# The expert loop in another order: each expert's down projection behind the next expert's gate and up

## The chip, the cores and the metric

The kernel runs on one core of a Trainium2 chip, as one launch. The metric is the time of one execution on the device in microseconds (us). The time of the kernel before is the median of three runs.

## The reference

One step of a small encoder trunk for two request groups (256 prompt frames and 32 sample frames, 288 tokens of 1024 features). It has two layers: an mLSTM and retention mixer, then a mixture of experts; a gated DeltaNet mixer, then a second mixture of experts. The change touches the two mixtures alone:

```python
def hier_moe(x, w_grp, b_grp, w_exp, b_exp, w_gate, w_up, w_down):
    """x (N,D): top-1 expert group, then top-2 experts inside it; only selected experts are evaluated."""
    ...
    def expert_block(args):
        xb, e = args
        hb = jax.nn.silu(xb @ w_gate[e]) * (xb @ w_up[e])
        return hb @ w_down[e]
    ...
    y = out_rows[dest] * gw_s[:, None].astype(x.dtype)
    return jax.ops.segment_sum(y, tok_s, num_segments=n)
```

There are 32 experts. Each has a gate and an up matrix of 1024 x 512 and a down matrix of 512 x 1024, all in float32, so each matrix is 2048 KB and each mixture reads 96 of them from device memory.

## The kernel before

**Blocks.** Tokens are held in slots of 32 per expert (`BLK`), and a block `b` is four experts (`QUAD`), numbered 4b to 4b+3. With the inputs of this case a mixture is eight blocks, each expert once. In the text expert 31 is the last of a mixture, and `u` is an expert's place in its block. The first block is written out, the others are a loop on each engine.

**TensorE (PE), for each block.** `gather` picks the block's token rows with one-hot products. Then for each of four experts: `gate_up(u, b)` multiplies 32 tokens by the gate and the up matrix (32 products each, it begins when both matrices are there); `flip_hidden(u, b)` transposes the hidden rows; `down(u, b)` multiplies by the down matrix (16 products). `scatter(b)` adds the block's rows to the tokens with five groups of products, and DVE adds them into `X`. Between `gate_up` and `flip_hidden` ScalarE (ACT) takes the SiLU and VectorE (DVE) multiplies by up (`hidden`); between `flip_hidden` and `down` DVE copies the flipped rows (`hidden_T`). After `down`, DVE and ACT copy the result to `ys` (`outputs`).

**The matrices.** Six ring slots of 2048 KB hold the matrices of two experts: expert i+2 is loaded into the slots of expert i (`RING_SLOT`; the first three experts have further slots, `FIRST_SLOT`). The loads are issued by SyncE's queue (SP), in program order: gate, up, down of one expert, then of the next. Each waits until its slot is read: on `gate_used`, `up_used` or `down_used`, which PE raises at the end of the gate half, of `gate_up` and of `down`.

**The ends of a mixture.** A mixture ends with `down(3, 7)`, its `outputs`, `scatter(7)` and DVE's adds. The first mixture is followed by the second layer's norm and input products, whose first four weight pieces SP loads into ring slots right behind expert 31's matrices (`pieces`). The second mixture is followed by the final norm and the stores.

**Where the first block differs.** In block 0 PE has `share_rows`, three products that spread the routing rows, behind the first `down`; DVE makes the next block's one-hot and this block's shares (`onehot(0)`, `shares(0)`) behind the first expert. In the trace the 32-wide hidden tiles are named `zT`, ring slots `W`, and PE's products stand at line 343, a helper.

Of the kernel before, what the change touches and what calls it, by code (L numbers as in the profile page):

```python
# [16 lines left out]
ACT = mybir.ActivationFunctionType  # L17
X_AXIS = mybir.AxisListType.X

P = 128  # L20
# [11 lines left out]
BLK = 32  # L32
QUAD = 4
# [104 lines left out]
def trunk(nc, a):  # L138

    with ExitStack() as ctx:  # L140
# [200 lines left out]
        def _(pe):  # L341
# [696 lines left out]
            def experts(l):  # L1038
# [148 lines left out]
                def expert(u, b):  # L1187
                    gate_up(u, b)
                    flip_hidden(u, b)
                    down(u, b)  # L1190
# [23 lines left out]
        def _(act):  # L1214
# [295 lines left out]
            def experts(l):  # L1510
# [34 lines left out]

                def iteration(b):
                    fetched(b)
                    for u in range(QUAD):
                        i = 4 * b + u
                        act.wait_ge(m["gate_used"], i + 3)  # L1550
                        nc.scalar.activation(sg[u % 2], banks[2 + u % 2][0:64, 0:2 * P], ACT.Silu  # L1551
                                             ).then_inc(m["silu"], 1)
                        act.wait_ge(m["down_used"], i + 3)
                        if u == 0:
                            act.wait_ge(m["scattered"], SCATTERS * b + SCATTERS)
                        for c in (2, 3):
                            ins = nc.scalar.copy(ys[BLK * u:BLK * u + BLK, 256 * c:256 * c + 256],  # L1557
                                                 banks[5 + u % 2][BLK * c:BLK * c + BLK, 0:256])
                            ins.then_inc(m["y_act"] if c == 3 else part_done, 1)
# [21 lines left out]
        def _(dve):  # L1581
# [710 lines left out]
            def experts(l):  # L2292
# [133 lines left out]
                def expert(u, b):  # L2426
                    i = 4 * b + u
                    hidden(u, i)
                    hidden_T(u, i)
                    outputs(u, i)  # L2430

# [39 lines left out]
                expert(0, 0)  # L2471
                for t in range(TILES):
                    n, bank = N_TOK[t], banks[(4, 6, 7)[t]]
                    E["rows_wide"].wait(dve)
                    cp(rows[:, :, P * t:P * t + n], bank[:, 0:4 * n].rearrange("p (j n) -> p j n", j=4))
                onehot(0)
                shares(0)
                for u in range(1, QUAD):
                    expert(u, 0)
                adds(0)  # L2480
                nb = nblk_reg(dve)
                with dve.Fori(1, nb) as b:
                    fetched(b)
                    expert(0, b)
# [345 lines left out]
```

## Time and profile before

| | |
|---|---|
| median of three runs | 1464.29 us (1462.56 to 1466.79) |
| the profiled execution, its own time | 1455.58 us |
| its span, from first to last instruction | 1453.7 us |
| PE busy | 1155.0 us (79%) |
| DVE busy | 470.4 us (32%) |
| ACT busy | 252.1 us (17%) |
| queue of SP's loads | 448.35 MB, 76.7% of 16 DMA engines |
| PE's mean granted clock | 0.903 |

The profiled execution is 8.7 us below the median of the three runs; sums are made against its own time. Busy shares are means over stages with different limits: the two mixtures and the two mixers have to be read apart, and a busy PE is not a PE at its peak, since products are pipelined and four narrow ones run side by side. The granted clock has two levels here, 1.00 (2.4 GHz) and 0.50 (1.2 GHz); a stretch that holds both shows a mean between them.

### The profile page before, as it was taken

What the parts mean: (1) busy time and instruction counts of PE and PEld (TensorE: products, weight loads), DVE (VectorE), ACT (ScalarE), POOL (GpSimd) and SP (SyncE); (2) the same over time, 40 slices, a digit from 0 to 9 for tenths busy, and PEclk for the clock granted to TensorE, in tenths of its full rate; (3) what the DMA queues carried; (4) which work ended last, traced back from release to release, by engine and by line L of the source; (5) the groups of instructions that cost most, each with busy time, mean ns of one, the idle gap of its engine ahead of it and who ended that gap; (6) DMA issues with size and microseconds to landing.
All of it is one profiled execution on the core that took longest, in us unless ns stands there. A gap on an engine that the chain in (4) does not pass through costs nothing.

```text
span 1453.7 us, 27532 instructions
## 1 busy us (share of the span) xinstructions
PE 1155.0 (79%) x11710; PEld 716.8 (49%) x11710; DVE 470.4 (32%) x1210; ACT 252.1 (17%) x636; POOL 65.7 (5%) x100
## 2 busy tenths in 40 slices
PE   8999889887686775776899989898866768778665
PEld 6645547444353443443578666656534434344342
DVE  1024355432232221322343746535222213222133
ACT  2122214110010110101222414231110101011011
POOL 2001102100000000000200101011000000000001
PEclk9999999988787898887999999898999978788898
DMA  9852236999999999999833303148999999999995
GB/s 278 171 105 81 109 123 249 424 410 428 428 427 430 427 429 429 428 429 427 277 117 116 118 4 131 60 182 341 410 427 429 428 428 429 427 430 428 428 429 218
DMA packets 54146, 453.87 MB, mean 312 GB/s; under 512 B 5680, under 2 KB 6480, under 8 KB 29760
## 3 DMA queue, kind: packets, MB, share of 16 engines
q1 hardware_dynamic: 52176, 448.35, 76.7%
q0 software_dynamic: 1904, 4.58, 1.1%
q8 instruction: 49, 0.80, 0.2%
q14 instruction: 17, 0.14, 0.0%
HBM read 449.55 MB, written 3.35 MB: 312 GB/s over the span
## 4 chain that ended last, share of the span: by engine, by line
PE 57%; DMA 31%; DVE 6%; issue 3%; ACT 1%; SPq 1%; POOL 1%; DVEq 0%; ACTq 0%; POOLq 0%
PE bank L343 56%; DMA W<-in_moe_w_up 30%; PE bank L346 1%; DMA W<-in_ab_w_in 1%; DVE zT L2402 1%; ACT zT L1551 1%; SPq L2554 1%; DVE zT L2407 1%; DVE HT L1586 0%; DVE zT L2412 0%; DVE W L1586 0%; DVE HN L1586 0%; DVE gain L1586 0%; DVE zT L1586 0%; DVE W L1606 0%
## 5 line engine op out<-in xcount | busy, mean ns | idle before, releaser
L343 PE MATMUL bank<-W,zT 128*32 128x256 f32 (+1 forms) x6272 | 517.5, 459 | 163.3 <-DMA W<-in_moe_w_up 137.2
L343 PEld LDWEIGHTS bank<-W,zT 128*32 128x32 f32 (+1 forms) x6272 | 253.1, 128 | 384.1 <-issue 266.9
L2402 DVE TENSOR_TENSOR zT<-zT,bank 64x256 f32<-64x256 f32 x64 | 27.0, 422 | 399.3 <-ACT zT L1551 399.3
L343 PE MATMUL bank<-W,HT 128*32 128x128 f32 (+1 forms) x768 | 133.5, 395 | 2.5 <-ACT TM L1288 2.3
L343 PE MATMUL bank<-HT,W 128*128 128x288 f32 x512 | 126.9, 408 | 3.2 <-DMA W<-in_ab_w_in 3.2
L343 PEld LDWEIGHTS bank<-HT,W 128*128 128x128 f32 x512 | 96.4, 190 | 30.0 <-DMA W<-in_ab_w_in 3.7
L2412 DVE COPY zT<-bank 32x256 f32<-32x256 f32 x128 | 53.3, 416 | 164.4 <-PE bank L343 162.4
L343 PE MATMUL bank<-const,zT 64*128 64x64 f32 (+3 forms) x340 | 47.9, 290 | 68.7 <-DVE zT L2402 68.3
L343 PEld LDWEIGHTS bank<-zT,HN 128*128 128x128 f32 (+1 forms) x832 | 95.7, 190 | 9.5 <-issue 8.3
L343 PE MATMUL bank<-zT,HN 128*128 128x128 f32 (+1 forms) x832 | 98.1, 276 | 1.2 <-DVE HN L1586 0.9
L1557 ACT COPY zT<-bank 32x256 f32<-32x256 f32 x128 | 46.8, 366 | 272.1 <-PE bank L343 270.6
L1551 ACT ACTIVATE zT<-bank 64x256 f32<-64x256 f32 x64 | 24.2, 378 | 385.3 <-PE bank L343 385.3
L343 PEld LDWEIGHTS bank<-W,HT 128*32 128x32 f32 (+1 forms) x768 | 61.4, 141 | 57.3 <-issue 53.2
L343 PEld LDWEIGHTS bank<-const,zT 64*128 64x128 f32 (+2 forms) x340 | 37.4, 173 | 101.9 <-DVE zT L2402 78.2
L343 PE MATMUL bank<-zT,HT 128*32 128x256 f32 (+1 forms) x256 | 68.3, 496 | 16.4 <-DVE zT L2412 16.4
L343 PEld LDWEIGHTS bank<-zT,HT 128*32 128x32 f32 (+1 forms) x256 | 26.0, 148 | 56.0 <-issue 56.0
L1542 ACT ACTIVATE zT<-bank,gcol 128x128 f32<-128x128 f32 x64 | 18.3, 369 | 157.3 <-PE bank L343 157.3
L2443 DVE TENSOR_TENSOR X<-X,bank 128x512 f32<-128x512 f32 x64 | 40.3, 685 | 0.5
L2633 POOL TENSOR_SCALAR sm<-sm 128x1 f32<-128x1 f32 (+3 forms) x21 | 5.7, 272 | 684.0 <-ACT zT L1220 470.2
L343 PE MATMUL bank<-W 32*32 32x32 f32 (+3 forms) x1352 | 28.5, 207 | 9.2 <-DVEq L1601 5.1
L2407 DVE COPY zT<-bank 128x128 f32<-128x128 f32 x64 | 18.7, 292 | 50.8 <-PE bank L343 50.8
L343 PEld LDWEIGHTS bank<-W 32*32 32x32 f32 (+3 forms) x1352 | 24.8, 119 | 19.0 <-DVEq L1601 9.4
(283 smaller groups left out, 867.9 us busy)
## 6 DMA issues: line engine op xcount, KB each, us to landing
W<-in_moe_w_gate SPq DMA_DIRECT2D x62, 2048.0 KB, 17.9
W<-in_moe_w_up SPq DMA_DIRECT2D x62, 2048.0 KB, 22.3
W<-in_moe_w_down SPq DMA_DIRECT2D x62, 2048.0 KB, 22.4
W<-in_ab_w_in SPq DMA_DIRECT2D x8, 2048.0 KB, 17.0
W<-in_c_w_in SPq DMA_DIRECT2D x8, 2048.0 KB, 13.5
W<-in_ab_w_out SPq DMA_DIRECT2D x2, 2048.0 KB, 7.7
TM<-in_moe_w_gate SPq DMA_DIRECT2D x2, 2048.0 KB, 16.6
zT<-in_moe_w_up SPq DMA_DIRECT2D x2, 2048.0 KB, 15.6
```

What stands on the lines that cost most here:

```text
L343: return nc.tensor.matmul(out, lhsT, rhs, start=start, stop=stop)
L346: return nc.tensor.transpose(out, src, ident[:n, :n])
L1542: nc.scalar.activation(xg[:, k, :], banks[1][:, (k - 4) * P:(k - 3) * P], ACT.Copy, scale=gcol[:, 4 + l, k:k + 1]).then_inc(m["xg_act"] if ...
L1551: nc.scalar.activation(sg[u % 2], banks[2 + u % 2][0:64, 0:2 * P], ACT.Silu).then_inc(m["silu"], 1)
L1557: ins = nc.scalar.copy(ys[BLK * u:BLK * u + BLK, 256 * c:256 * c + 256], banks[5 + u % 2][BLK * c:BLK * c + BLK, 0:256])
L2402: v.tensor_tensor(hid[u % 2], sg[u % 2], banks[2 + u % 2][64:128, 0:2 * P], ALU.mult).then_inc(m["hidden"], 1)
L2407: v.tensor_copy(hidT[u % 2], banks[4][:, 0:P]).then_inc(m["hiddenT"], 1)
L2412: ins = v.tensor_copy(ys[BLK * u:BLK * u + BLK, 256 * c:256 * c + 256], banks[5 + u % 2][BLK * c:BLK * c + BLK, 0:256])
L2443: v.tensor_tensor(x, x, banks[(5, 6, 7, 4)[i]][:, :], ALU.add).then_inc(m["added"], 1)
L2554: sp.dma_start(slots[k], flat).then_inc(moe[l]["w_in"][k], 16)
L2633: do(nc.gpsimd.tensor_scalar(src, src, scale, EPS, ALU.mult, ALU.add))
```

## The change

PE gives the products another order: `down(u)` stands behind the next expert's `gate_up`. In block 0 and in the loop the order is not quite alike. SP issues the loads from block 2 on in a like order; those of blocks 0 and 1 stand as they were. ACT takes the next expert's SiLU ahead of each copy of outputs. DVE's pieces follow PE's order, and in block 0 `onehot(0)` and `shares(0)` stand behind the third expert's `hidden_T`.

```diff
@@ PE @@
-                expert(0, 0)
+                gate_up(0, 0)
+                gate_up(1, 0)
+                flip_hidden(0, 0)
+                down(0, 0)
                 share_rows()
-                for u in range(1, QUAD):
-                    expert(u, 0)
+                gate_up(2, 0)
+                flip_hidden(1, 0)
+                down(1, 0)
+                flip_hidden(2, 0)
+                gate_up(3, 0)
+                down(2, 0)
+                flip_hidden(3, 0)
+                down(3, 0)
                 scatter(0)
...
                     gather(b)
-                    for u in range(QUAD):
-                        expert(u, b)
+                    gate_up(0, b)
+                    gate_up(1, b)
+                    flip_hidden(0, b)
+                    down(0, b)
+                    flip_hidden(1, b)
+                    gate_up(2, b)
+                    down(1, b)
+                    flip_hidden(2, b)
+                    gate_up(3, b)
+                    down(2, b)
+                    flip_hidden(3, b)
+                    down(3, b)
                     scatter(b)
@@ ACT @@
-                    for u in range(QUAD):
...
+                    silu(0, b)
+                    for u in range(1, QUAD):
+                        silu(u, b)
+                        outputs(u - 1, b)
+                    outputs(QUAD - 1, b)
@@ DVE, first block @@
-                expert(0, 0)
+                hidden(0, 0)
+                hidden_T(0, 0)
+                outputs(0, 0)
...
+                hidden(1, 1)
+                hidden_T(1, 1)
+                hidden(2, 2)
+                outputs(1, 1)
+                hidden_T(2, 2)
                 onehot(0)
                 shares(0)
-                for u in range(1, QUAD):
-                    expert(u, 0)
+                hidden(3, 3)
+                hidden_T(3, 3)
+                outputs(2, 2)
+                outputs(3, 3)
                 adds(0)
@@ DVE, loop @@
                     fetched(b)
-                    expert(0, b)
+                    hidden(0, 4 * b)
                     onehot(b)
                     shares(b)
-                    for u in range(1, QUAD):
-                        expert(u, b)
+                    hidden(1, 4 * b + 1)
+                    hidden_T(0, 4 * b)
+                    outputs(0, 4 * b)
+                    hidden_T(1, 4 * b + 1)
+                    hidden(2, 4 * b + 2)
+                    outputs(1, 4 * b + 1)
+                    hidden_T(2, 4 * b + 2)
+                    hidden(3, 4 * b + 3)
+                    hidden_T(3, 4 * b + 3)
+                    outputs(2, 4 * b + 2)
+                    outputs(3, 4 * b + 3)
                     adds(b)
@@ SP, from block 2 on @@
                 with sp.Fori(2, nb) as b:
                     for u in range(QUAD):
-                        load_next(b, u, 4 * b + u + 1)
+                        load_gate_up(b, u, 4 * b + u + 1)
+                        if u:
+                            load_down(b, u - 1, 4 * b + u)
+                    load_down(b, QUAD - 1, 4 * b + QUAD)
```

On SP, this is the end of the loop's body before, from the third expert's down load on; the loop line follows, and behind it in the first mixture the next layer's pieces.

```order
L2554 DMA W<-in_moe_w_down 128x4096 [waits moe0_down_used]
L2592 ISA
L2592 TENSOR_LOAD blocks_i
L2592 ISA x2
L2594 REGISTER_ALU
L2554 ISA [waits moe0_gate_used]
L2554 DMA W<-in_moe_w_gate 128x4096
L2554 DMA W<-in_moe_w_up 128x4096 [waits moe0_up_used]
L2554 DMA W<-in_moe_w_down 128x4096 [waits moe0_down_used]
```

And the same end now, from the fourth expert's gate load on.

```order
L2586 ISA [waits moe0_gate_used]
L2586 DMA W<-in_moe_w_gate 128x4096
L2586 DMA W<-in_moe_w_up 128x4096 [waits moe0_up_used]
L2626 TENSOR_LOAD blocks_i
L2626 ISA x2
L2586 ISA [waits moe0_down_used]
L2586 DMA W<-in_moe_w_down 128x4096
L2626 TENSOR_LOAD blocks_i
L2626 ISA x2
L2586 ISA [waits moe0_down_used]
L2586 DMA W<-in_moe_w_down 128x4096
```

The last up matrix now has two down matrices behind it in the queue, the third and the fourth expert's, where it had one.

On PE, this is the end of the loop's body before: the third expert's `down` (bank5), the fourth expert's `gate_up` (bank3), `flip_hidden` (bank4) and `down` (bank6), and the first product of `scatter`.

```order
L343 MATMUL bank5<-W,zT 32x256 [waits moe0_y_dve,moe0_y_act,moe0_w_in1,moe0_hiddenT]
L343 MATMUL bank5<-W,zT 32x256 x15
L1108 REGISTER_ALU
L343 MATMUL bank3<-W,zT 32x256 [waits moe0_w_in3,moe0_w_in2]
L343 MATMUL bank3<-W,zT 32x256 x31
L1132 REGISTER_ALU
L343 MATMUL bank4<-const,zT 128x64 [waits moe0_hidden]
L343 MATMUL bank4<-const,zT 128x64
L343 MATMUL bank6<-W,zT 32x256 [waits moe0_y_dve,moe0_y_act,moe0_w_in4,moe0_hiddenT]
L343 MATMUL bank6<-W,zT 32x256 x15
L343 MATMUL bank4<-zT,HT 32x256 [waits moe0_y_act,moe0_y_dve,moe0_share]
```

And the same end now.

```order
L343 MATMUL bank3<-W,zT 32x256 [waits moe0_w_in3,moe0_w_in2]
L343 MATMUL bank3<-W,zT 32x256 x31
L343 MATMUL bank5<-W,zT 32x256 [waits moe0_y_dve,moe0_y_act,moe0_w_in1,moe0_hiddenT]
L343 MATMUL bank5<-W,zT 32x256 x15
L1132 REGISTER_ALU
L343 MATMUL bank4<-const,zT 128x64 [waits moe0_hidden]
L343 MATMUL bank4<-const,zT 128x64
L343 MATMUL bank6<-W,zT 32x256 [waits moe0_y_dve,moe0_y_act,moe0_w_in4,moe0_hiddenT]
L343 MATMUL bank6<-W,zT 32x256 x15
L343 MATMUL bank4<-zT,HT 32x256 [waits moe0_y_act,moe0_y_dve,moe0_share]
```

The third expert's `down` has moved from ahead of the fourth expert's `gate_up` to between it and its flip.

On PE in block 0, this is the difference from the first expert's flip (bank4) to the second expert's `down` (bank6), before and then now; `bank4`, `bank6` and `bank7` from `HT` are `share_rows`, and `TM` is the third expert's gate matrix.

```order
L343 MATMUL bank4<-const,zT 128x64 [waits moe0_added,moe0_hidden]
L343 MATMUL bank4<-const,zT 128x64
L343 MATMUL bank5<-W,zT 32x256 [waits moe0_w_in4,moe0_hiddenT]
L343 MATMUL bank5<-W,zT 32x256 x15
L343 MATMUL bank4<-HT,const 128x512 [waits rows_diag]
L343 MATMUL bank6<-HT,const 128x512 [waits rows_diag]
L343 MATMUL bank7<-HT,const 128x128 [waits rows_diag]
L343 MATMUL bank3<-W,zT 32x256 [waits moe0_w_in0,moe0_w_in5]
L343 MATMUL bank3<-W,zT 32x256 x31
```

```order
L343 MATMUL bank3<-W,zT 32x256 [waits moe0_w_in0,moe0_w_in5]
L343 MATMUL bank3<-W,zT 32x256 x31
L343 MATMUL bank4<-const,zT 128x64 [waits moe0_added,moe0_hidden]
L343 MATMUL bank4<-const,zT 128x64
L343 MATMUL bank5<-W,zT 32x256 [waits moe0_w_in4,moe0_hiddenT]
L343 MATMUL bank5<-W,zT 32x256 x15
L343 MATMUL bank4<-HT,const 128x512 [waits rows_diag]
L343 MATMUL bank6<-HT,const 128x512 [waits rows_diag]
L343 MATMUL bank7<-HT,const 128x128 [waits rows_diag]
L343 MATMUL bank2<-TM,zT 32x256 [waits extra_in1,extra_in0]
```

The second expert's `gate_up` (bank3) now stands ahead of the first expert's flip, and so ahead of its `down`.

## Rows read from the trace of the kernel before

**Rows 1.** The page's span in 40 equal slices, what the DMA engines moved.

```profile
GB/s 278 171 105 81 109 123 249 424 410 428 428 427 430 427 429 429 428 429 427 277 117 116 118 4 131 60 182 341 410 427 429 428 428 429 427 430 428 428 429 218
```

**Rows 2.** One stretch by engine: busy us (instructions), PE's clock, DMA share, GB/s.

```profile
400.00:460.00 60.00, 45.84 (x488) 26.01 (x484) 14.00 (x33) 5.58 (x16) 0.00 (x0) 0.81 1.01 429
```

**Rows 3.** PE's waits over the span: us in total, times, longest.

```profile
PE bank L343 <- DMA W<-in_moe_w_up: 137.2, 33, 7.0
PE bank L343 <- DVE zT L2402: 68.3, 64, 2.6
```

**Rows 4.** Timeline, PE, end of the second mixture, from expert 31's `gate_up`.

```profile
1430.32 5.12 PE L343 MATMUL bank<-W,zT 128*32 128x256 f32 x64 [5.08 <-DMA W<-in_moe_w_up]
...
1436.45 0.68 PE L343 MATMUL bank<-const,zT 64*128 64x64 f32 x4 [1.01 <-DVE zT L2402]
...
1437.52 1.93 PE L343 MATMUL bank<-W,zT 128*32 128x256 f32 x32 [0.38 <-DVE zT L2407]
...
1440.49 4.27 PE L343 MATMUL bank<-zT,HT 128*32 128x256 f32 x16 [1.04 <-DVE zT L2412]
```

**Rows 5.** Timeline, PE, end of the first mixture and the next layer's first product.

```profile
691.12 6.03 PE L343 MATMUL bank<-W,zT 128*32 128x256 f32 x64 [3.01 <-DMA W<-in_moe_w_up]
...
699.22 1.93 PE L343 MATMUL bank<-W,zT 128*32 128x256 f32 x32 [0.38 <-DVE zT L2407]
...
713.91 4.05 PE L343 MATMUL bank<-HT,small_w 128*16 128x288 f32 x16 [0.91 <-DVEq L1601]
```

**Rows 6.** Timeline of SP's queue: five issues of loads.

```profile
671.88 0.33 SPq L2554 DMA_DIRECT2D W<-in_moe_w_down  x1
...
1002.77 0.43 SPq L2554 DMA_DIRECT2D W<-in_moe_w_up  x1
1009.46 0.33 SPq L2554 DMA_DIRECT2D W<-in_moe_w_down  x1
...
1049.45 0.33 SPq L2554 DMA_DIRECT2D W<-in_moe_w_gate  x1
...
1408.84 0.33 SPq L2554 DMA_DIRECT2D W<-in_moe_w_down  x1
```

**Rows 7.** DMA issues at 671.88, 1002.77 and 1408.84: size, us to landing.

```profile
W<-in_moe_w_down SPq DMA_DIRECT2D x1, 2048.0 KB, 24.0
...
W<-in_moe_w_up SPq DMA_DIRECT2D x1, 2048.0 KB, 13.3
...
W<-in_moe_w_down SPq DMA_DIRECT2D x1, 2048.0 KB, 26.2
```

**Rows 8.** Two stretches in the columns of rows 2: a `down`, a `gate_up`.

```profile
1006.00:1009.50 3.50, 3.42 (x33) 1.53 (x33) 0.07 (x2) 0.04 (x1) 0.00 (x0) 0.57 0.99 417
...
1415.60:1421.30 5.70, 5.60 (x64) 2.82 (x64) 0.00 (x0) 0.03 (x1) 0.00 (x0) 0.66 1.01 428
```

**Rows 9.** Timeline, PE, second mixture: block 0's beginning, and a later `gate_up`.

```profile
998.54 3.83 PE L343 MATMUL bank<-W,zT 128*32 128x256 f32 x64
...
1005.02 0.68 PE L343 MATMUL bank<-const,zT 64*128 64x64 f32 x4 [2.65 <-DVE zT L2402]
...
1006.08 3.33 PE L343 MATMUL bank<-W,zT 128*32 128x256 f32 x32 [0.38 <-DVE zT L2407]
...
1400.95 3.84 PE L343 MATMUL bank<-W,zT 128*32 128x256 f32 x64 [1.44 <-DMA W<-in_moe_w_up]
```

**Rows 10.** Two stretches of 2 us, second mixture: PE clock, DMA share, GB/s last.

```profile
1048.00:1050.00 2.00, 1.27 (x24) 0.47 (x16) 0.18 (x1) 0.38 (x1) 0.00 (x0) 1.00 0.82 344
1050.00:1052.00 2.00, 1.24 (x16) 0.94 (x20) 0.53 (x2) 0.00 (x0) 0.00 (x0) 1.00 1.00 279
```

**Rows 11.** Timeline, PE, between two blocks: `scatter`, `gather`, the next `gate_up`.

```profile
1382.05 4.27 PE L343 MATMUL bank<-zT,HT 128*32 128x256 f32 x16 [1.04 <-DVE zT L2412]
...
1386.15 5.52 PE L343 MATMUL bank<-zT,HN 128*128 128x128 f32 x48
...
1391.61 3.83 PE L343 MATMUL bank<-W,zT 128*32 128x256 f32 x64
```

More of the change, by code:

```diff
@@ L1544, in fetched, with silu, outputs @@
                                              ).then_inc(m["xg_act"] if k == 7 else part_done, 1)
+                def silu(u, b):
+                    act.wait_ge(m["gate_used"], 4 * b + u + 3)
+                    nc.scalar.activation(sg[u % 2], banks[2 + u % 2][0:64, 0:2 * P], ACT.Silu
+                                         ).then_inc(m["silu"], 1)
+                def outputs(u, b):
+                    act.wait_ge(m["down_used"], 4 * b + u + 3)
+                    if u == 0:
+                        act.wait_ge(m["scattered"], SCATTERS * b + SCATTERS)
+                    for c in (2, 3):
+                        ins = nc.scalar.copy(ys[BLK * u:BLK * u + BLK, 256 * c:256 * c + 256],
+                                             banks[5 + u % 2][BLK * c:BLK * c + BLK, 0:256])
+                        ins.then_inc(m["y_act"] if c == 3 else part_done, 1)
                 def iteration(b):
                     fetched(b)
-                    for u in range(QUAD):
[L1549 to L1559, printed above, removed]
+                    silu(0, b)
[3 more added lines that the diff above has]
+                    outputs(QUAD - 1, b)
                 iteration(0)
@@ L2424, in shares @@
                     dve.wait_ge(m["share_step"], 3 * b + 3)
[L2426 to L2430, printed above, removed]
                 def adds(b):
@@ L2539, in pieces @@
                         dma(hgain[:, 1, :], row(a["ab_norm_b"][0]), hgain_in)
[L2541 removed]
+            MATRICES = ("moe_w_gate", "moe_w_up", "moe_w_down")
             def expert_piece(l, k, s, e):
[L2545 to L2546 removed]
+                src = a[MATRICES[s]][l, bass.ds(e, 1), :, :]
                 flat = src.rearrange("o (p k) n -> p (o k n)", p=P)
@@ L2584, in experts, with listed, load_gate_up, load_down @@
                 first(2, 2)
-                for s in range(3):
-                    sp.wait_ge(m[LOADS[s][1]], 3)
-                    first(3, s)
-                E["blocks_ready"].wait(sp)
-                def load_next(b, u, done):
-                    e = sp.value_load(blocks_i[0:1, bass.ds(4 * b + u, 1)], min_val=0, max_val=NEXP - 1)
-                    for s in range(3):
-                        sp.wait_ge(m[LOADS[s][1]], done)
-                        expert_piece(l, RING_SLOT[u % 2][s], s, e)
+                sp.wait_ge(m["gate_used"], 3)
+                first(3, 0)
+                sp.wait_ge(m["up_used"], 3)
+                first(3, 1)
+                sp.wait_ge(m["down_used"], 3)
+                first(3, 2)
+                E["blocks_ready"].wait(sp)
+                def listed(b, u):
+                    return sp.value_load(blocks_i[0:1, bass.ds(4 * b + u, 1)], min_val=0, max_val=NEXP - 1)
+                def load_gate_up(b, u, done):
+                    e = listed(b, u)
+                    sp.wait_ge(m["gate_used"], done)
+                    expert_piece(l, RING_SLOT[u % 2][0], 0, e)
+                    sp.wait_ge(m["up_used"], done)
+                    expert_piece(l, RING_SLOT[u % 2][1], 1, e)
+                def load_down(b, u, done):
+                    e = listed(b, u)
+                    sp.wait_ge(m["down_used"], done)
+                    expert_piece(l, RING_SLOT[u % 2][2], 2, e)
                 for u in range(QUAD):
-                    load_next(1, u, u + 5 if u else 4)
+                    load_gate_up(1, u, u + 5 if u else 4)
+                    load_down(1, u, u + 5 if u else 4)
                 nb = nblk_reg(sp)
```

7 lines of the change are left out of this document (removed).

## The prediction

> **What bounds the kernel.** I read the slices first. The DMA engines move 410 to 430 GB/s in two long plateaus, twelve slices and eleven, of 36.3 us each (1453.7 / 40), which are the two mixtures; elsewhere they idle [rows 1]. One stretch inside a plateau says what sets the pace there: 429 GB/s at a DMA share of 1.01, with PE busy for 45.84 of 60 us [rows 2]. A matrix of 2048 KB is 2.097 MB and takes 2.097 / 0.429 = 4.89 us, an expert 14.7 us, whatever PE does. PE's waits agree: 137.2 us are spent on an up matrix, 33 times, and 68.3 us on DVE's `hidden`, 64 times, 1.07 us each [rows 3]. The change hides the second kind behind products of the next expert. Inside the plateau that is worth nothing: PE reaches the next up matrix earlier and waits there longer, so the cover of the gain is the stream itself. It can count only where the stream isn't the limit: behind the last transfer, and where a transfer was issued late. So I then read the ends of both mixtures, and SP's issues against landings.
>
> **The end of a mixture, before.** Expert 31's down matrix is the last to land: issued at 1408.84 and 26.2 us under way, at 1435.0 in the second mixture; at 671.88 + 24.0 = 695.9 in the first [rows 6, 7]. Its `down` begins at 1437.52 and 699.22 [rows 4, 5], 2.5 and 3.3 us after the matrix is there. What is late is the chain from the up matrix: it lands one transfer, 4.9 us, ahead of the down matrix, and from there stand `gate_up` of 5.12 us (6.03 in the first mixture), 1.01 us to the flip, 0.68 us of flip and 0.38 us to `down` [rows 4, 5]. That is 7.2 and 8.1 us against 4.9.
>
> **The end, after.** Up 31 now has down 30 and down 31 behind it, so it lands 9.8 us ahead of the last matrix. PE's work in that time is `gate_up` 31 (5.12 or 6.03), `down` 30 (1.93), flip 31 (0.68) and the 0.38 us to `down` 31: 8.1 or 9.0 us. The 1.01 us of SiLU and `hidden` lie behind `down` 30. Both are under 9.8, so `down` 31 starts as its matrix lands, and the 2.5 and 3.3 us go: 5.8 us together. What follows `down` (outputs, `scatter`, adds) keeps its order and length. DVE's `outputs` of expert 30 stand behind `hidden_T` 31 in its queue now, and are done in the pause before the last matrix. In the first mixture the gain must also pass into the second layer. Its first product at 713.91 waits for DVE's norm, not for a weight piece [rows 5], and piece loads follow down 31 in the queue as before; so I let it pass in full.
>
> **A cost there: PE's clock.** The last `down` now follows a pause. It lasts 9.8 - 8.1 + 0.38 = 2.1 us or, with the longer `gate_up`, 1.2 us. Pauses of both kinds are in the trace. After a wait of 1.44 us a `gate_up` took 3.84 us, its full-speed length; after one of 2.65 us, with a short flip between, a `down` took 3.33 us where it takes 1.93 [rows 9, 4], and that stretch had a granted clock of 0.57, mostly the lower level of 1.2 GHz [rows 8]. So a slow last `down` costs 3.33 - 1.93 = 1.40 us. The two pauses lie between 1.44 and 2.65 or just under; I count one slow `down` of the two, -1.4, and keep 0 and 2.8 as the bounds.
>
> A rule bears on this. The Trainium skill, in "TensorE: Matmul & The Clock Gate", section "HAM oscillation — how this bites in real kernels", describes a loop whose products are shorter than the DMA wait: every wait lets the clock fall, and the next products start cold. The rows agree for the long waits (the `gate_up` at 1415.6 ran at a mean clock of 0.66 [rows 8]) and not for the one of 1.44 us. Applied to both last `down`s it makes the sum 5.8 - 2.8 here instead of 5.8 - 1.4.
>
> **Late issues in block 0.** In the second mixture the gate load at 1049.45 [rows 6] waits for `gate_up` 4, PE's first product behind block 0, and the DMA engines fall to 344 and 279 GB/s in the 4 us around it [rows 10]. Against 429 that loses 2 x (85 + 150) / 429 = 1.1 us. With the change PE leaves block 0 earlier. The second expert's `gate_up` (3.83 us) covers the first flip's wait of 2.65 us and keeps the clock up, so the first `down` needs 1.93 instead of 3.33 us; the other experts' 1.07 us mostly go too: 2.65 + 1.40 + 2 x 1.07 = 6.2 us [rows 3, 9], of which I take 4 to 5, since DVE's row copies and `share_rows` now stand ahead of the second flip. Issued at about 1045, the load is behind a full queue. I take 1.0 us; the bounds are 0 and 1.1. In the first mixture I count nothing: its block 0 begins while its first loads still run.
>
> One load there comes under threat: down 3, issued at 1009.46 when the first `down` ends, which now waits for `gate_up` 1 as well. That puts its end at 998.54 + 3.83 + 3.83 + 0.68 + about 0.4 + 1.93 = 1009.2, no later than before, because of the faster clock; at the lower clock 1010.6. Up 3, ahead of it in the queue, lands at 1002.77 + 13.3 = 1016.1 [rows 7], so some 5 us are spare. SP's further gate loads wait in its queue behind down 3, and they are freed earlier, by `gate_up` 1. The moved one-hot and shares (DVE, block 0) are needed at `scatter` and `gather`, after the fourth expert; nothing waits. SP's added list reads cost nothing, since SP waits anyway for slots between its issues.
>
> **Sum.** 5.8 - 1.4 + 1.0 = 5.4 us, 0.37%. On the profiled execution's own time that is 1455.58 - 5.4 = 1450.2; the median of the runs shown lies 8.7 us higher, and with no part of that tied to the ends of the mixtures I carry the difference over: 1464.29 - 5.4 = 1458.9. From the bounds the gain is between 5.8 - 2.8 + 0 = 3.0 and 5.8 + 1.1 = 6.9, so 1457.4 to 1461.3 for this case. A change of under 0.3%, 4.4 us, is about what a measurement of this kernel can't tell from none.
>
> **Rivals.**
>
> *Both last `down`s at the lower clock, or more of the end with them.* For it: the clock falls after waits of 2.65 us and more, and the new pause is on the edge. Against it: the pause comes right behind 7 us of dense products. Gain 5.8 - 2.8 + 1.0 = 4.0, time 1460.3, within 0.3%. If `scatter` (4.27 us [rows 4]) starts low as well, some 1.5 us more are lost per mixture, and the gain is about 1: 1463.3. Chance 0.28. The rule cited above from the Trainium skill, "TensorE: Matmul & The Clock Gate", would make the first of these times the likeliest.
>
> *The change does nothing at the ends.* The stream ends when it ended, and the gain at the first end is swallowed by the next layer, whose weight pieces land when they did. For it: the four pieces are bound to the stream, not to PE. Against it: the first product there waits for DVE. Gain 2.5 + 0 to 1 - 1.4, about 1.5: 1462.8. Chance 0.06.
>
> *Slower: the gate of a slot comes too late at a block's beginning.* Between two blocks PE has `down`, 1.04 us of outputs, `scatter`, `gather` and `gate_up` of the new block's first expert before that gate slot is free: 1.93 + 1.04 + (1391.61 + 3.83 - 1382.05 = 13.4) = 16.4 us after the last down matrix lands [rows 4, 11]. In the old load order six transfers, 29.4 us, lie between that landing and the load that needs the slot; in the new one five, 24.5 us, since the first expert's down comes later. The margin shrinks from 13 to 8 us, less 3.5 us from issue to flow (13.3 - 2 x 4.89 for the load at 1002.77 on idle engines [rows 7]). It decides if that chain grows by over 4.6 us, which would take most of it at the lower clock. For it: the clock does fall in the loop, 0.81 on the mean [rows 2]. Against it: these three groups are dense, and 5.52 and 3.83 us are their full-speed lengths. Twelve such boundaries (blocks 2 to 7, twice) at 1 us each past that point are +12, less the 5.4: 1470.9. Chance 0.06.
>
> **Numbers.** The forecast has 0.60, the first rival 0.28, the second 0.06, the third 0.06. Two thirds of the forecast's 3.0 to 6.9 lie past 4.4 us, and its likeliest part, so 0.45 of the 0.60 counts as faster; the runs' own spread (4.2 us over the three) lifts some 0.10 of what lies just under 4.4 over the bound: faster 0.55, same 0.39, slower 0.06. The range must hold the forecast and most of the first two rivals, and the spread of a median by some 2 us: 1454.5 to 1464.5.
>
> **What will show it.** Right: in both mixtures `down` 31 starts within 0.3 us of its matrix's landing (before 2.5 and 3.3); the wait on DVE's `hidden` falls from 68.3 us to under 20, that on the up matrix grows by about as much; the stream stays at 428 to 430 GB/s; the gate load behind block 0 in the second mixture is issued some 5 us earlier, and the dip around it is gone. Wrong: a `down` 31 of 3 us or a `scatter` of more than 5; a DMA dip of 2 us or more at the blocks' beginnings; a first layer-two product that comes no earlier after the last landing. A gain of over 8 us would mean that the stream itself got faster, which no row here allows for.

## The result and the profile after

| | median | lowest to highest | runs |
|---|---|---|---|
| before | 1461.64 us | 1452.37 to 1469.59 | 18 |
| after | 1451.90 us | 1445.31 to 1461.35 | 18 |

The ratio is 0.994, 95% interval 0.9924 to 0.9956: 8.8 us less (6.4 to 11.1). A second comparison, below, gave 0.9961 (0.9937 to 0.9985). Weighted by their intervals the two give 0.9946 plus or minus 0.0013, or 7.8 us less (5.9 to 9.8). Single executions of one kernel spread over 16 to 17 us, twice the effect. The profiled one of the changed kernel took 1458.29 us, more than the profiled one of before (1455.58), so the two spans must not be subtracted; they have to be compared stage by stage.

PE's waits in the changed kernel, as in [rows 3]:

```profile
PE bank L343 <- DMA W<-in_moe_w_up: 211.5, 40, 9.0
...
PE bank L343 <- DVE zT L2428: 17.0, 26, 1.2
```

The wait on DVE's `hidden`, 68.3 us in 64 pieces before, is gone as a group (the row of line 2428 is the wait on `hidden_T`), and the wait on an up matrix grew by 211.5 - 137.2 = 74.3 us. Inside the stream the gain was given back, as forecast. The slices of DMA throughput stand at the old height:

```profile
GB/s 283 170 100 90 99 123 153 425 411 427 428 430 428 429 428 429 428 429 428 354 122 118 118 3 103 89 140 349 424 427 423 428 430 427 431 426 431 426 431 232
```

The end of the second mixture (timeline, PE), as in [rows 4]. Rows of one form are joined: the 96 products are `gate_up` 31 and `down` 30.

```profile
1428.89 7.02 PE L343 MATMUL bank<-W,zT 128*32 128x256 f32 x96 [6.56 <-DMA W<-in_moe_w_up]
1435.84 0.68 PE L343 MATMUL bank<-const,zT 64*128 64x64 f32 x4
...
1438.62 3.44 PE L343 MATMUL bank<-W,zT 128*32 128x256 f32 x32 [2.10 <-issue]
...
1443.07 4.27 PE L343 MATMUL bank<-zT,HT 128*32 128x256 f32 x16 [1.02 <-DVE zT L2433]
```

The end of the first, as in [rows 5]:

```profile
694.42 7.34 PE L343 MATMUL bank<-W,zT 128*32 128x256 f32 x96 [6.28 <-DMA W<-in_moe_w_up]
701.69 0.68 PE L343 MATMUL bank<-const,zT 64*128 64x64 f32 x4
...
704.18 2.88 PE L343 MATMUL bank<-W,zT 128*32 128x256 f32 x32 [1.81 <-issue]
...
708.08 6.07 PE L343 MATMUL bank<-zT,HT 128*32 128x256 f32 x16 [1.01 <-DVE zT L2433]
```

The issue of the last matrix in the second mixture (timeline of SP's queue), and its size and us to landing (DMA issues):

```profile
1421.92 0.33 SPq L2586 DMA_DIRECT2D W<-in_moe_w_down  x1
...
W<-in_moe_w_down SPq DMA_DIRECT2D x1, 2048.0 KB, 16.6
```

By the trace's landing events the last matrices arrive at 1438.53 and 704.09, so the last `down` starts 0.09 us behind each; before, it was 2.5 and 3.3. But here both `down`s, and one `scatter` (6.07 instead of 4.27), ran slow. The prediction lists a `down` 31 of 3 us and a `scatter` of more than 5 among its signs of being wrong; the second mixture shows the one, the first the other. The granted clock was 1.00 over the pause and 0.54 over the `down` behind it (stretches in the columns of rows 2; the third last figure is the granted clock):

```profile
1436.50:1438.60 2.10, 0.02 (x1) 0.01 (x1) 1.13 (x3) 0.23 (x1) 0.00 (x0) 1.00 0.19 78
1438.60:1442.10 3.50, 3.44 (x32) 1.71 (x32) 0.00 (x0) 0.00 (x0) 0.00 (x0) 0.54 0.00 0
```

At block 0 of the second mixture SP issues (first, up 3; last, the gate load that [rows 6] show at 1049.45):

```profile
1007.38 0.43 SPq L2586 DMA_DIRECT2D W<-in_moe_w_up  x1
1013.63 0.33 SPq L2586 DMA_DIRECT2D W<-in_moe_w_down  x1
...
1046.23 0.33 SPq L2586 DMA_DIRECT2D W<-in_moe_w_gate  x1
```

From up 3 to that gate it is 38.9 us now and was 1049.45 - 1002.77 = 46.7 [rows 6]: 7.8 us earlier. The dip of [rows 10] is gone:

```profile
1046.00:1048.00 2.00, 0.06 (x4) 0.00 (x0) 1.37 (x4) 0.38 (x1) 0.00 (x0) 1.00 0.97 418
1048.00:1050.00 2.00, 0.00 (x0) 0.00 (x0) 1.97 (x6) 0.00 (x0) 0.00 (x0) 0.94 1.00 426
```

### The profile page after: what moved, and what is told of

Read it like the earlier page. It is cut to its first block, busy times and chain, and to the rows that moved or that the text cites. A ratio compares the mean times of both kernels' runs of the same rounds, so it can differ in the third digit from the quotient of the medians.

```text
span 1456.3 us, 27754 instructions
## 1 busy us (share of the span) xinstructions
PE 1144.0 (79%) x11710; PEld 723.3 (50%) x11710; DVE 471.0 (32%) x1210; ACT 251.4 (17%) x636; POOL 65.4 (4%) x100
## 4 chain that ended last, share of the span: by engine, by line
PE 49%; DMA 42%; DVE 4%; issue 3%; ACT 1%; SPq 1%; POOL 0%; DVEq 0%; ACTq 0%; POOLq 0%
PE bank L343 48%; DMA W<-in_moe_w_up 41%; PE bank L346 2%; SPq L2586 1%; DMA X<-in_x_prompt 0%; DVE W L1607 0%; DVE HN L1607 0%; DVE gain L1607 0%; DVE HT L1607 0%; DVE W L1627 0%; DVE HN L1627 0%; POOL sm L2681 0%; DVE zT L2428 0%; ACT TM L1470 0%; DVE gain L1619 0%
## 5 line engine op out<-in xcount | busy, mean ns | idle before, releaser
L343 PE MATMUL bank<-W,zT 128*32 128x256 f32 (+1 forms) x6272 | 503.4, 450 | 245.2 <-DMA W<-in_moe_w_up 211.5
L343 PEld LDWEIGHTS bank<-W,zT 128*32 128x32 f32 (+1 forms) x6272 | 258.4, 127 | 448.6 <-issue 340.7
L343 PE MATMUL bank<-zT,HN 128*128 128x128 f32 (+1 forms) x832 | 101.3, 281 | 1.2 <-DVE HN L1607 0.9
L343 PE MATMUL bank<-zT,HT 128*32 128x256 f32 (+1 forms) x256 | 73.9, 537 | 16.4 <-DVE zT L2433 16.4
L1570 ACT COPY zT<-bank 32x256 f32<-32x256 f32 x128 | 46.6, 364 | 151.1 <-PE bank L343 149.5
L2452 DVE TENSOR_TENSOR X<-X,bank 32x256 f32<-32x256 f32 x64 | 26.5, 415 | 15.6 <-PE bank L343 14.1
## 6 DMA issues: line engine op xcount, KB each, us to landing
W<-in_ab_w_in SPq DMA_DIRECT2D x8, 2048.0 KB, 16.3
```

What stands on the lines that cost most here:

```text
L343: return nc.tensor.matmul(out, lhsT, rhs, start=start, stop=stop)
L2452: ins = v.tensor_tensor(x, x, banks[4][32 * q:32 * q + 32, 0:256], ALU.add)
```

## The experiments

Each profile is cut into stages, all from trace events. **Stream 1, 2**: from the landing of expert 3's gate matrix to that of expert 31's down, in each mixture. **End 1, 2**: from there to the end of DVE's last add. **Mixer 2**: from the last add of mixture 1 to the first SiLU of mixture 2. All in us; ratios are to the kernel before on the same chip. The stages of a row come from one profile, a ratio from a dozen or more executions.

| kernel | stream 1 | end 1 | mixer 2 | stream 2 | end 2 | ratio [95%] |
|---|---|---|---|---|---|---|
| before | 425.1 | 11.29 | 295.2 | 424.6 | 10.44 | |
| before, second profile | 426.0 | 11.93 | 294.1 | 425.5 | 10.50 | |
| before, third | 426.1 | 12.19 | 295.1 | 426.3 | 10.75 | |
| after | 424.4 | 10.78 | 292.1 | 422.9 | 9.54 | 0.9940 [0.9924, 0.9956] |
| after, second | 425.6 | 9.55 | 291.3 | 422.9 | 10.78 | 0.9961 [0.9937, 0.9985] |
| after, third | 424.9 | 8.05 | 295.4 | 423.4 | 10.78 | |
| block 0 alone | 426.0 | 10.66 | 295.9 | 422.9 | 10.64 | 0.9987 [0.9963, 1.0012] |
| loop alone | 426.7 | 8.04 | 294.2 | 427.8 | 8.04 | 0.9959 [0.9942, 0.9975] |
| old loads | 425.3 | 12.22 | 292.5 | 422.9 | 11.17 | 0.9991 [0.9971, 1.0011] |
| 8 idle products | 428.2 | 8.94 | 293.1 | 424.8 | 8.47 | 0.9981 [0.9961, 1.0001] |
| block 1's loads | 426.0 | 8.04 | 291.2 | 422.9 | 8.04 | 0.9956 [0.9935, 0.9977] |
| block 1's loads and 4 idle products | 425.8 | 8.04 | 292.4 | 422.5 | 8.04 | 0.9958 [0.9941, 0.9974] |
| before, delayed | 424.5 | 10.66 | 294.3 | 427.2 | 10.75 | 1.0025 [0.9999, 1.0051] |
| after, delayed | 426.1 | 8.05 | 297.1 | 424.1 | 8.05 | 0.9963 [0.9939, 0.9987] |

**Block 0 alone.** The changed block 0 with the old loop on PE, ACT and DVE and the old loads; the diff is to the changed kernel, PE and SP.

```diff
                     gather(b)
-                    gate_up(0, b)
-                    gate_up(1, b)
-                    flip_hidden(0, b)
...
+                    for u in range(QUAD):
+                        gate_up(u, b)
+                        flip_hidden(u, b)
+                        down(u, b)
                     scatter(b)
...
                         load_gate_up(b, u, 4 * b + u + 1)
-                        if u:
-                            load_down(b, u - 1, 4 * b + u)
-                    load_down(b, QUAD - 1, 4 * b + QUAD)
+                        load_down(b, u, 4 * b + u + 1)
```

> The first block in the new order on PE, ACT and DVE; the loop and its loads as before. The change as a whole measured 0.994 of before (about -9 us) where -5.4 was forecast. Theory A, the first block was mis-sized: PE's clock falls there in most executions, slots come free late and the stream stalls by 3 to 5 us over both mixtures, not by 1.0. Then this kernel alone gives a ratio of 0.9965 to 0.998 (-3 to -5 us), and its two streams, from the fourth expert's gate landing to the last down, are 421 to 423 us where before has 425. Theory B, the ends were mis-sized: this kernel gives at most -1.5 us (0.999 or nearer to 1), with the last down 2 to 3.5 us behind its matrix as before.

Stream 2 is 422.9 us, the changed kernel's, and the ends are the old ones. Stream 1, at 426.0, is not shorter, so of theory A's two streams only the second bears it out. The time, 1.9 us less (5.4 less to 1.8 more), lies between the two theories and doesn't tell by itself.

**Loop alone.** The other half: the old block 0 on PE, ACT and DVE, the new loop and loads; again against the changed kernel, PE.

```diff
-                gate_up(0, 0)
-                gate_up(1, 0)
-                flip_hidden(0, 0)
-                down(0, 0)
+                expert(0, 0)
                 share_rows()
-                gate_up(2, 0)
...
+                for u in range(1, QUAD):
+                    expert(u, 0)
                 scatter(0)
```

> The first block as before on all engines, its one-hot and shares too; the loop and its loads in the new order. Theory A (the first block holds the missing gain): -4 to -5.5 us, ratio 0.996 to 0.9975, last downs start within 0.3 us of the landing, the streams stay at 424 to 426 us. Theory B (the ends hold it): -7.5 to -9 us, ratio 0.994 to 0.995.

6.0 us less (3.7 to 8.5): most of the gain, and just beyond theory A's range. Both ends are at 8.04. Stream 2 is not shortened; at 427.8 it is 2.3 us longer than the mean of the three profiles of before, and outside the expected 424 to 426. Some 1.5 us of that is the gate matrix of block 2's third expert, which landed that much late. In this one profile the ends give 6.3 us and the streams take back 3.3, so the stages show 3.0 of the 6.0. The timed halves add up, 1.9 + 6.0 = 7.9 against 7.8 for the whole, but with intervals of over 2 us either way that is no test of it.

**Old loads.** The whole change, with SP's loads in the old order.

```diff
                         load_gate_up(b, u, 4 * b + u + 1)
-                        if u:
-                            load_down(b, u - 1, 4 * b + u)
-                    load_down(b, QUAD - 1, 4 * b + QUAD)
+                        load_down(b, u, 4 * b + u + 1)
```

> Everything as changed, but SP issues gate, up and down of one expert together, as before. At the ends the last up then lands one transfer (4.9 us) ahead of the last down, and PE has gate_up, down of the third expert, flip and down behind it: 5.1 to 6.0 + 1.9 + 0.7 + 0.4 = 8.1 to 9.0 us, so the last down starts 3.2 to 4.1 us behind its matrix, about 1 us later than before at each end. Theories A and B: the first block's gain less about 2 us, A about -2 us (0.9985), B about +1 us. A third theory, C, that the order of the products alone matters, since PE hides its waits in every block: about as the change, -8 to -9 us.

Timeline, PE, end of the first mixture:

```profile
696.75 8.03 PE L343 MATMUL bank<-W,zT 128*32 128x256 f32 x96 [7.15 <-DMA W<-in_moe_w_up]
704.71 0.68 PE L343 MATMUL bank<-const,zT 64*128 64x64 f32 x4
705.77 1.93 PE L343 MATMUL bank<-W,zT 128*32 128x256 f32 x32 [0.38 <-DVE zT L2428]
```

The matrix landed at 701.52, so the last `down` is 4.2 us late, and 3.2 in the second mixture: later than before, since `down` 30 now stands in its way. PE's new order without the loads' lengthens the ends by 1.0 us together over the mean of before. The gain at the ends comes from the up matrix landing one transfer earlier. The time, 1.3 us less than before (4.2 less to 1.6 more), is near theory A's and speaks against theory C, by which the order of the products alone would give 8 to 9.

**8 idle products.** The whole change, with 8 idle products (16 passes) ahead of each block's last `down`, to keep the clock up.

```diff
                     flip_hidden(3, b)
+                    idle_products(8, 0)
                     down(3, b)
```

> The change with 8 idle products (128 columns, about 1.4 us at the full clock) on PE between the last flip and the last down of each block of the loop, so that the pause before the last down doesn't lower the clock. In the profile of the changed kernel the last downs took 2.88 and 3.44 us, and one scatter 6.07, where 1.93 and 4.27 are the full-speed lengths. If the clock at the ends matters: last downs of 1.93 us, and 2 to 4 us faster than the changed kernel over both ends, ratio to before about 0.992. If the clock falls through other gaps, or the idle products themselves run late: no difference from the changed kernel (0.994).

Timeline, PE, end of the first mixture:

```profile
700.42 0.68 PE L343 MATMUL bank<-const,zT 64*128 64x64 f32 x4
701.03 2.05 PE L343 MATMUL bank<-const 128*128 128x128 f32 x16
703.02 1.93 PE L343 MATMUL bank<-W,zT 128*32 128x256 f32 x32
```

The `down` is short, but 0.97 us behind its matrix (702.05): the idle products took 2.05 us, not the 1.4 expected. Both streams are longer than the changed kernel's, and in them the gate load of block 2's third expert landed 2.2 and 1.7 us later than one transfer behind the load ahead of it. That is the third rival's place, reached by an experiment that delays the last `down` by hand. With 2.8 us less than before (5.7 less to 0.1 more) the kernel meets neither of the times expected, 0.992 and 0.994.

**Again; block 1's loads; 4 idle products.** The changed kernel and the kernel before again; the change with block 1's loads in the new order too; and that with 4 idle products. All four were measured on one chip.

```diff
                     load_gate_up(1, u, u + 5 if u else 4)
-                    load_down(1, u, u + 5 if u else 4)
+                    if u:
+                        load_down(1, u - 1, u + 4 if u > 1 else 4)
+                load_down(1, QUAD - 1, QUAD + 4)
...
                     flip_hidden(3, b)
+                    idle_products(4, 0)
                     down(3, b)
```

> The changed kernel once more, beside the two below on one chip, for its ratio and a second profile. Ratio to before 0.993 to 0.996. Theory A (first block of the second mixture): its stream from the fourth gate's landing to the last down is again 422.5 to 423.5 us there; the ends, 8.0 to 10.8 us from the last landing to the last add, as PE's clock falls.

> The kernel before, a second profile. Theory A: its stream in the second mixture is 424 to 428 us, with loads of the first two blocks landing late, and its ends are 10.4 to 11.3 us each. Theory B (the ends hold what was missing): ends well over 11.3.

> The change with block 1's loads in the new order too (before the change and after it they stand gate, up, down of one expert). In two experiments with the new loop a gate load of expert 10 landed 0.8 to 2.2 us late, since block 1 still ends as before: its last down waits for the up behind it. Theory of that late load: none at expert 10 any more; 0 to 1.5 us faster than the changed kernel on the mean (ratio 0.992 to 0.995), as the changed kernel's own profile shows no such stall. Rival, that the stall came from the clock alone: no difference.

> The kernel above with 4 idle products, half as many as in e4 (there they took 2.05 us and made the last down 0.97 us late), between the last flip and the last down of each block of the loop: 1.0 us. Theory, the clock at the ends costs on the mean 1.1 us per end (8.04 at best against 9.1 on the mean of four): last downs of 1.93 us, ends of 8.0 to 8.6 us, 1 to 2 us faster than the kernel above (ratio 0.991 to 0.994). Rival: the clock falls anyway or the idle products cost as much: no difference.

With block 1's loads moved, the end of the second mixture is the forecast's best case (the wait is put down to DVE, but DVE's copy was done 0.6 us earlier, and the matrix landed 0.09 us before the `down`):

```profile
1417.81 8.19 PE L343 MATMUL bank<-W,zT 128*32 128x256 f32 x96 [6.99 <-DMA W<-in_moe_w_up]
1425.93 0.68 PE L343 MATMUL bank<-const,zT 64*128 64x64 f32 x4
1427.52 1.93 PE L343 MATMUL bank<-W,zT 128*32 128x256 f32 x32 [0.91 <-DVE zT L2428]
```

All three versions beat the kernel before; among them 0.9956, 0.9958 and 0.9961 can't be told apart, so neither edit is shown to add anything. The late gate load of expert 10 is gone with block 1's loads moved, as that theory says, but the changed kernel's own profiles hadn't shown it. The 4 idle products gave two ends of 8.04 us, and no time. In the second profile of before, end 1 (11.93) lies over the expected 11.3, because the last `down` ran slow there too (timeline, PE):

```profile
699.81 3.20 PE L343 MATMUL bank<-W,zT 128*32 128x256 f32 x32 [0.38 <-DVE zT L2407]
```

**Delayed.** 12 idle products (24 passes) behind block 0's `scatter`, in the kernel before and in the changed one; and a third profile of each. All were measured on one chip.

```diff
                 scatter(0)
+                idle_products(12, 0)
```

> The kernel before, with 12 idle products (24 passes, estimated at 3.1 us from 16 passes of 2.05 us in the run with 8) on TensorE behind block 0's scatter, ahead of the loop: everything that block 0 releases and the loop's first block come about 3 us later. Theory A (in the second mixture the old block 0 ends so near the running dry of the load queue that each us by which it ends later is lost by the stream of matrices, though its own work is hidden): the stretch from the landing of the fourth gate matrix to that of the last down grows from 424.6 to 426.0 us in the profiles of the kernel before to 427 to 429; time +2 to +4 us, ratio 1.0015 to 1.003. Rival B (block 0's end is hidden, and only the two ends of the loop gave the gain): stretch 424.6 to 426.5, ratio 0.999 to 1.001.

> The changed kernel with the same 12 idle products behind block 0's scatter. Theory A: block 0 releases its buffers some us before the queue runs dry, so about 3 us more are covered: the stretch from the fourth gate's landing to the last down's stays at 422.5 to 423.5 us in the second mixture, and the ratio to before at 0.994 to 0.997, as without them. Rival B says the same of this kernel; a stretch of 425 or more would say that the new block 0 stands at the same edge as the old one, and that its gain came from elsewhere.

> The kernel before once more, for a third profile. If the stages found so far are the kernel's own: stretch of the second mixture 424.5 to 426 us, each mixture's last add 10.4 to 12 us behind the last matrix, second mixer 294 to 296 us.

> The changed kernel once more, for a third profile. If the stages found so far are the change's own: stretch of the second mixture 422.5 to 423.2 us, last add 8 to 10.8 us behind the last matrix, second mixer 291 to 292.5 us. A second mixer of 294 us or more would say that its difference of 2.7 us between the kernels is chance.

The delay in the kernel before is 1044.29 - 1041.62 = 2.67 us (timeline, PE):

```profile
1041.62 2.84 PE L343 MATMUL bank<-const 128*128 128x128 f32 x24
1044.29 5.52 PE L343 MATMUL bank<-zT,HN 128*128 128x128 f32 x48
```

These are the issues of its up 3 and of the gate behind block 0, and then the dip (columns of rows 2):

```profile
1004.43 0.43 SPq L2555 DMA_DIRECT2D W<-in_moe_w_up  x1
...
1053.76 0.33 SPq L2555 DMA_DIRECT2D W<-in_moe_w_gate  x1
```

```profile
1050.00:1052.00 2.00, 2.00 (x40) 1.15 (x36) 0.00 (x0) 1.00 (x4) 0.00 (x0) 1.00 0.73 311
1052.00:1054.00 2.00, 1.59 (x28) 0.65 (x20) 0.00 (x0) 0.38 (x1) 0.00 (x0) 1.00 0.10 41
1054.00:1056.00 2.00, 0.93 (x11) 0.71 (x15) 0.71 (x2) 0.00 (x0) 0.00 (x0) 1.00 0.79 172
1056.00:1058.00 2.00, 2.00 (x27) 0.99 (x22) 0.00 (x0) 0.00 (x0) 0.00 (x0) 0.53 0.84 352
```

Against 429 GB/s that loses 2 x (118 + 388 + 257 + 77) / 429 = 3.9 us. The kernel before itself, in its third profile, without any delay:

```profile
1011.99 0.43 SPq L2554 DMA_DIRECT2D W<-in_moe_w_up  x1
...
1060.12 0.33 SPq L2554 DMA_DIRECT2D W<-in_moe_w_gate  x1
```

```profile
1058.00:1060.00 2.00, 1.95 (x36) 0.87 (x28) 0.00 (x0) 0.02 (x1) 0.00 (x0) 1.00 0.68 279
1060.00:1062.00 2.00, 0.68 (x4) 0.54 (x4) 0.66 (x2) 0.36 (x1) 0.00 (x0) 1.00 0.76 139
1062.00:1064.00 2.00, 1.90 (x20) 1.03 (x24) 0.05 (x1) 0.00 (x0) 0.00 (x0) 0.58 0.79 328
```

2 x (150 + 290 + 101) / 429 = 2.5 us. And the changed kernel, delayed:

```profile
1002.53 1.16 SPq L2587 DMA_DIRECT2D W<-in_moe_w_up  x1
...
1044.06 0.33 SPq L2587 DMA_DIRECT2D W<-in_moe_w_gate  x1
```

```profile
1044.00:1046.00 2.00, 0.00 (x0) 0.00 (x0) 1.54 (x5) 0.30 (x1) 0.00 (x0) 1.00 1.09 467
1046.00:1048.00 2.00, 0.96 (x16) 0.66 (x20) 1.83 (x5) 0.00 (x0) 0.00 (x0) 0.88 0.96 410
```

No dip. Set against the time from up 3's issue to that gate's, worked out in the same way for every profile:

| profile | up 3 to gate | lost in the dip |
|---|---|---|
| loop alone | 46.6 us | 1.2 us |
| before | 46.7 us | 1.1 us |
| before, second | 46.7 us | 1.4 us |
| before, third | 48.1 us | 2.5 us |
| before, delayed | 49.3 us | 3.9 us |
| after, three profiles | 38.9 us | none |
| after, delayed | 41.5 us | none |

From 46.7 to 49.3 us the loss rises from 1.2 us, the mean of the first three rows, to 3.9, about one us for each us of block 0. A straight line through these rows would begin near 45.5 us; that is an estimate, since no profile lies between 41.5 and 46.6. The changed kernel stands over 6 us short of it. So theory A holds: the old block 0 ended at the edge where its release decides the stream. The rival, by which only the ends gained, expected at most 426.5 us of stream 2 in the delayed kernel before and fails at 427.2, though not by much: an undelayed profile had 426.3. The dips are the clearer sign. In the first mixture the same delay left stream 1 at 424.5, so the edge is the second mixture's alone, as forecast. The timed ratio, 1.0025, agrees with theory A but its interval reaches 0.9999. The delayed changed kernel's stream 2 is 424.1, over the 423.5 expected: down 3 landed 0.87 us late there, and it is issued ahead of the delay.

The other values of the third profiles lie near what was expected: stream 2 at 426.3 before and 423.4 after, and end 1 at 12.19 before, each 0.2 to 0.3 us over its range. Mixer 2 looked 2.7 us shorter in kernels with the new loop until these last profiles; 295.4 and 297.1 in two of them say, by the sign set ahead, that this is chance. Its length goes with the clock granted in it: 0.98 in the changed kernel's profiles of 292.1 and 291.3 us, 0.96 to 0.97 in those of 294.1 to 295.4 (the other one of after and the three of before), 0.95 in the one of 297.1. Why the clock differed isn't known.

## Why the prediction was off

The direction, the main mechanism and its place were right; the time lay 2.6 us under the range. The forecast was 1458.9 us, the measured median 1451.9, 7.0 less. Two steps failed: the base that the gain was taken from (2.65 us), and the term for late issues in block 0, which was put at 1.0 us with an upper bound of 1.1 and measured 2.4. The 2.9 us that remain of the 7.0 can't be given to a step.

**The base: 2.65 us.** "The median of the runs shown lies 8.7 us higher, and ... I carry the difference over" took 1464.29 from three runs. Over 18 runs the kernel before has 1461.64. The median of three executions of a kernel whose executions spread over 17 us couldn't carry a forecast to 0.2%. Taken from 1461.64, the same range would begin at 1451.85, just under the measured median.

**Late issues in block 0: the term that was mis-sized.** "I take 1.0 us; the bounds are 0 and 1.1." The mechanism is shown above, and the gate was issued 7.8 us earlier, not 5. Block 0 had four waits on `hidden`, of 2.65, 0.98, 0.92 and 0.93 us, and the slow `down` with 1.40; all five are gone, 6.9 us. The forecast counted 6.2 of this and then took off 1.2 to 2.2 for DVE's row copies and `share_rows` ahead of the second flip, where nothing was lost: the flip follows the third `gate_up` without a wait. But 1.1 us was the dip of one execution, and a mild one: three executions of before lost 1.1, 1.4 and 2.5 us. Stream 2 as a whole went from a mean of 425.5 (424.6 to 426.3) to 423.1 (422.9 to 423.4): 2.4 us. The dip's mean, 1.7 us, is most of that; where the other 0.7 lies was not taken apart. "A gain of over 8 us would mean that the stream itself got faster, which no row here allows for": it did get faster, by this term, and [rows 10] did allow for it. The upper bound should have been asked as what a slightly later block 0 would lose, not as what this one lost.

**The ends: right, with the clock costing more in some executions.** The lateness taken away was 5.8 us by one profile; the three profiles of before have ends 3.1 us longer on the mean than 8.04, the shortest end of any profile, 6.3 us for two. A part of that is the clock's too: in two of these six ends (the first mixture of the second and third profile) the last `down` took 3.20 and 3.44 us. In every profile with the new order of products and loads, and without idle products, the last `down` starts 0.09 us behind its matrix. The price of the clock was put at 1.4, one slow `down` of two, by a pause of 2.1 us or, with a longer `gate_up`, 1.2. Here are all twelve ends of this kind (six profiles: the changed kernel's three, its delayed form, the loop alone, block 1's loads):

| profile, mixture | `gate_up` 31 and `down` 30 | pause | last `down` |
|---|---|---|---|
| after, second, 1 | 6.78 us | 2.38 us | 3.43 us |
| after, 2 | 7.02 | 2.10 | 3.44 |
| after, third, 2 | 7.26 | 1.83 | 2.93 |
| after, 1 | 7.34 | 1.81 | 2.88 |
| after, second, 2 | 7.46 | 1.64 | 2.50 |
| loop alone; after delayed (two each) | 7.95 to 8.16 | 0.94 to 1.22 | 1.93 |
| after, third, 1 | 8.12 | 1.04 | 1.94 |
| block 1's loads (two) | 8.19, 8.34 | 0.91, 0.81 | 1.93 |

Five of twelve are slow, near the one in two that was counted. What the forecast's sum left out, and its first rival named, is that `scatter` can follow at the lower clock (6.0 to 6.5 us instead of 4.27 in three of those five): the five cost 1.5 to 2.7 us each, 1.9 us per execution over the twelve. The Trainium skill, in "TensorE: Matmul & The Clock Gate", section "HAM oscillation — how this bites in real kernels", describes a loop whose products are shorter than the wait for DMA, with each wait letting the clock fall and the next products starting cold. The ends are not quite that loop, since 7 to 8 us of products stand ahead of a pause of at most 2.4; the `down`s behind pauses of 1.64 us and more did start cold, those behind 1.22 and less did not. That the pause matters is shown by the idle products: where they filled it, wholly or in part, all four `down`s took 1.93 us, one of them behind 7.11 us of `gate_up` 31 and `down` 30. That it isn't all is shown by the two slow ends of before, behind waits of 1.00 and 0.38 us. The changed kernel's own three profiles had five slow ends of six, so in them the ends gained only 22.37 - 19.83 = 2.5 us, near the 3.0 of the first rival; the variants with the same code at the ends had none of six. The timed ratios of the change and of the one with block 1's loads do not differ, which speaks for chance; whether it is chance stays open.

**Passing into the second layer: right.** The norm's first product came 18.0, 19.1 and 19.5 us behind the last matrix before, and 16.9, 16.3 and 15.2 after.

**The cover inside the stream: right.** PE's waits changed places, as the rows above show. **The slot at a block's beginning: did not decide.** In the changed kernel's three profiles no gate load at that place landed late; behind block 1 of the second mixture a single load did, the up of expert 12 in the third profile, by 0.65 us. With the old block 0 (loop alone) the gate of block 2's third expert landed 0.8 and 1.5 us late, with 8 idle products 2.2 and 1.7. So the place is real, but for one block of a mixture, not for six at 1 us. With block 1's loads in the new order too it was not late; why the old block 0 brings it about wasn't traced.

**The sum.** Over three profiles each, stream 2 gave 2.4 us, the ends 2.5, stream 1 0.8 (within its spread of 1 us, none was forecast), and mixer 2 1.9, which goes with the clock and is chance as far as it can be told. Of these, the stages that the forecast rests on make 4.9 us, under its 5.4. With the ends as all twelve show them, 6.3 - 1.9 = 4.4, they make 6.8. The timed halves say 6.0 (3.7 to 8.5) for the loop, forecast at 4.4, and 1.9 for block 0, forecast at 1.0. Of the 7.8 us measured over both comparisons, 2.4 more than forecast, the runs assign 1.4 to block 0's term; the last us is below what they resolve, and so is where the first comparison's further us came from. Whether that last us is luck can't be told.

## What to carry to other kernels

When a stream of transfers sets the pace, reordering the products behind it pays at its end and where its queue runs dry. At its end it pays only if the loads are reordered with the products: the order of products alone gave 1.3 us here (interval through none), with the loads' order 7.8. Where the queue ran dry the products' order was enough: stream 2 was 422.9 us with the old loads too. A small dip in the stream is a warning, not a size: ask how many us the work that releases it may slip, since past that edge each us cost about one here. And compare stages over several profiles before giving a size to a term of 1 us.

## What the runs showed of the hardware that was not expected

**The clock in a stage that nobody touched.** The first mixer, up to the first SiLU, is the same code in both kernels and took 259.6 us in one profile and 269.6 in another (259.6 to 268.7 over three of before, 260.4 to 269.6 over three of after). The columns are those of rows 2, the stretches stand at the same times from the start; in before:

```profile
150.00:170.00 20.00, 17.18 (x93) 10.08 (x92) 8.59 (x27) 6.57 (x20) 3.17 (x5) 1.00 0.34 119
170.00:200.00 30.00, 23.95 (x147) 13.66 (x146) 11.69 (x24) 4.73 (x16) 1.23 (x2) 0.94 0.36 141
200.00:240.00 40.00, 37.91 (x236) 22.78 (x235) 21.67 (x52) 12.30 (x31) 7.08 (x13) 1.00 0.23 79
```

And in the profiled execution of after:

```profile
150.00:170.00 20.00, 17.51 (x86) 9.78 (x84) 8.14 (x24) 6.29 (x20) 3.16 (x5) 0.91 0.34 119
170.00:200.00 30.00, 25.23 (x127) 14.96 (x128) 9.70 (x21) 4.31 (x16) 1.23 (x2) 0.77 0.36 140
200.00:240.00 40.00, 36.30 (x151) 20.58 (x150) 18.95 (x43) 5.08 (x22) 4.43 (x6) 0.91 0.05 14
```

The granted clock was 0.91, 0.77 and 0.91 where it had been 1.00, 0.94 and 1.00. (The slower execution falls behind, so the last stretch doesn't hold quite the same instructions.) Over the profiles the length goes with the clock granted from 150 us to the first SiLU: 0.97 and 0.95 in the two of 259.6 us, 0.94 in those of 260.4 to 261.1, 0.91 in that of 268.7, 0.89 in that of 269.6. This stage alone moved single profiles by more than the whole change; why the clock differs between executions of the same code isn't known.

**A low clock pays for itself.** At the ends, a `gate_up` that ran slow shortened the pause behind it, since the matrix lands when it lands, and the `down` behind the shorter pause ran at full speed. There the slow `gate_up` cost nothing, and the fast one cost up to 2.7 us.
